# Latents' projections ahead of the low-rank ones, and the recurrence's first seven rounds beside the last two row chunks

## The reference, cut to what matters

```python
h = rms_norm(x, mix_pre_norm) * (1 + sc_m) + sh_m     # x: 1024 tokens x 1024
proj = h @ w_in                                        # 456 attention columns, 1824 recurrent ones
# attention: latents c_q, c_kv, idx_k; score = sum_h w_h relu(q_h . k); keep the best 256 of each row
# recurrence: p + mu_shift * (p_prev - p), split into r, k, v and three low-rank inputs wd, ad, gd
w_log = -softplus(-(w0 + tanh(wd) @ w_decay_up)) - 0.5
a = sigmoid(a0 + ad @ w_aaa_up);  g = sigmoid(gd) @ w_gate_up
S = S * w_t + (S @ a_t) b_t + v_t k_t ;  y_t = S @ r_t          # 8 heads of 64 x 64, 1024 steps
```

## Time and profile before

| | before |
|---|---|
| times of three runs | 3676.62, 3683.32, 3688.82 us; median 3683.32 |
| profiled execution | 3676.93 us, span 3675.6 us |
| PE, DVE, ACT, POOL busy | 3362.3, 1789.6, 931.7, 345.4 us |
| mean granted clock | 0.957 of full |

### The profile page before, as it was taken

One profiled execution on the slowest core, in us unless ns is written; L12 is line 12 of the kernel. 1 busy time (PEld: TensorE's weight loads), 2 busy tenths in 40 slices (PEclk: granted clock), 3 DMA queues, 4 the chain that ended last, 5 costly groups with the idle time before them and its releaser, 6 DMA issues.

```text
span 3675.6 us, 51037 instructions
## 1 busy us (share of the span) xinstructions
PE 3362.3 (91%) x21635; PEld 2614.7 (71%) x21650; DVE 1789.6 (49%) x2849; ACT 931.7 (25%) x1710; POOL 345.4 (9%) x277
## 2 busy tenths in 40 slices
PE   6989757888889999999999889999998999999998
PEld 3757546765557788888886556876676888878876
DVE  2248878663566422223544546322246444444556
ACT  2146532332543300001112435000015111111122
POOL 0000156662000000000000000000000000000000
PEclk8999877988999999999999999999999999999999
DMA  6145411110024111112340101101123111123434
GB/s 210 41 68 183 155 36 37 37 60 19 13 75 138 58 46 52 46 50 94 107 140 25 36 24 35 46 21 49 57 98 117 55 47 46 52 69 98 143 113 145
DMA packets 216068, 270.18 MB, mean 74 GB/s; under 512 B 11068, under 2 KB 176226, under 8 KB 215587
## 3 DMA queue, kind: packets, MB, share of 16 engines
q1 hardware_dynamic: 210555, 247.87, 21.1%
q10 hardware_dynamic: 3192, 11.17, 1.7%
q0 software_dynamic: 2096, 7.87, 0.6%
HBM read 232.80 MB, written 34.08 MB: 73 GB/s over the span
## 4 chain that ended last, share of the span: by engine, by line
PE 80%; DVE 11%; ACT 3%; issue 3%; DMA 2%; POOL 1%; SPq 0%; DVEq 0%; ACTq 0%; POOLq 0%
PE psum L1977 18%; PE psum L1981 18%; PE psum L1979 18%; PE psum L508 5%; PE psum L2995 3%; PE psum L1181 2%; PE psum L2495 2%; PE psum L2816 2%; PE psum L2703 2%; PE psum L552 1%; PE psum L1727 1%; PE psum L2832 1%; DVE scores L913 1%; PE psum L1753 1%; DVE Lg L1821 1%
## 5 line engine op out<-in xcount | busy, mean ns | idle before, releaser
L1977 PE MATMUL psum<-hT_hi,wcut_lo 128*128 128x512 f32 x1856 | 589.9, 395 | 16.8 <-DVE hT_lo L2016 16.8
L1981 PE MATMUL psum<-hT_lo,wcut_hi 128*128 128x512 f32 x1856 | 582.8, 391 | 0.0
L1979 PE MATMUL psum<-hT_hi,wcut_hi 128*128 128x512 f32 x1856 | 582.6, 391 | 0.0
L1977 PEld LDWEIGHTS psum<-hT_hi,wcut_lo 128*128 128x128 f32 x1856 | 350.7, 189 | 97.2 <-DVE hT_lo L2016 17.9
L1959 DVE CAST wcut_hi<-raw 128x1024 fp32r<-128x1024 f32 x256 | 177.1, 692 | 477.0 <-PE psum L1981 453.0
L1979 PEld LDWEIGHTS psum<-hT_hi,wcut_hi 128*128 128x128 f32 x1856 | 350.7, 189 | 73.0
L1981 PEld LDWEIGHTS psum<-hT_lo,wcut_hi 128*128 128x128 f32 x1856 | 350.4, 189 | 73.4
L1977 PE MATMUL psum<-wcut_hi,xcut_lo 128*128 128x512 f32 x1120 | 347.3, 391 | 17.6 <-DVE xcut_lo L2095 13.8
L1981 PE MATMUL psum<-wcut_lo,xcut_hi 128*128 128x512 f32 x1120 | 346.5, 391 | 0.0
L1979 PE MATMUL psum<-wcut_hi,xcut_hi 128*128 128x512 f32 x1120 | 346.2, 390 | 0.0
L1035 POOL TENSOR_TENSOR st<-st,nhalf 128x1 f32<-128x1 f32 (+2 forms) x78 | 61.0, 789 | 2890.0 <-DVE st L676 2890.0
(11 more groups left out here) (427 smaller groups left out, 4396.8 us busy)
## 6 DMA issues: line engine op xcount, KB each, us to landing
raw<-in_w_ffn_down SPq DMA_DIRECT2D x88, 512.0 KB, 3.6
raw<-in_w_ffn_up SPq DMA_DIRECT2D x66, 512.0 KB, 3.8
slot<-in_ada_w SPq DMA_DIRECT2D x24, 1024.0 KB, 11.2
raw<-in_w_in SPq DMA_DIRECT2D x28, 512.0 KB, 5.3
raw<-in_w_ffn_gate SPq DMA_DIRECT2D x22, 512.0 KB, 3.9
slot<-in_w_in SPq DMA_DIRECT2D x8, 1024.0 KB, 6.4
raw<-in_w_out SPq DMA_DIRECT2D x16, 512.0 KB, 3.7
x_one<-xrow SPq DMA_DIRECT2D x16, 512.0 KB, 2.8
```

The source lines that it names most:

```text
L1977: pe.matmul(outs[i], al, bs[i][0], start=start, stop=False, skip_group_check=True)
L1979: pe.matmul(outs[i], ah, bs[i][0], start=False, stop=False, skip_group_check=True)
L1981: mm = pe.matmul(outs[i], ah, bs[i][1], start=False, stop=stop, skip_group_check=True)
```

## The change

The latents' projections now stand ahead of the low-rank ones. "lora" 0 is computed one matmul at a time between the first 16 score steps, "lora" 1 and 2 behind the scores, and DVE runs 30 passes of the search there (`LORA_PASSES`). All 16 modulation steps stand between ("rkv", 1, 5) and ("rkv", 3, 4), one behind each row step, with fixed slots. The last 16 row steps, chunks 4 and 5, have 2 passes each instead of 4, and rounds 0 to 6 of tile 0 stand behind every second of them (`round_beside`). The recurrence's loop begins at round 7. Its rows are loaded in two parts: r and k (`keys_load`), which need chunks 0 to 3 alone, and v (`values_load`). POOL's three operations on v move from a tile's round 1 to round 6 (round 8 for tile 0). The recurrence's constants move up, into `rwkv_weights` behind the load of chunk 4's weights. The last chunk is stored in two halves. Buffers lie elsewhere, so that round 0 can run while the stage buffers and the search are alive, and the attention's first loads all wait for the last inversion (T "U", 7).

```diff
+ROW_LOADS = [("mod", j, q) for j in (0, 1) for q in range(4)] + ["att a", "att b", ("rkv", 0), "idx q", ("rkv", 1), "lora a", "lora b",
+             ("rkv", 2)]
...
-        if _c < 5 and _t in (5, 6, 7)[:3 if _c < 4 else 2]:
-            ROW_STEPS.append(_mods.pop(0))
-ROW_STEPS += _mods
+        if (1, 5) <= (_c, _t) < (3, 5):
+            ROW_STEPS.append(_mods[sum(s[0] == "mod" for s in ROW_STEPS)])
+    _chunk_done.append(sum(s[0] == "mod" for s in ROW_STEPS))
...
+for _i, _s in enumerate(_mods):
+    ROW_LOADS.append(_s)
+    ROW_LOADS += [("rkv", _c + 3) for _c in range(3) if min(_chunk_done[_c] + 2, len(_mods)) == _i + 1]
+SLOT_OF = {_s: (1, 3, 4)[_i % 3] for _i, _s in enumerate(_mods)}
+SLOT_OF.update({("rkv", _c): 2 * (_c % 2) for _c in range(2, 6)})
...
+BESIDE = len(ROW_STEPS) - 2 * NT
...
-        if key == ("rkv", 3):
+        if key == ("rkv", 4):
             rwkv_weights(sp, K)
-        if key == ROW_LOADS[-1]:
-            rwkv_constants(sp, K)
+    rwkv_rows(sp, K)
...
     for n, (t, q) in enumerate(SCORES):
-        score_tensor(pe, K, t, q, SCORE_BANKS[n % 2])
+        score_tensor(pe, K, t, q, n)
+        if n < 16:
+            lora_tensor(pe, K, 0, n)
+    for m in (1, 2):
+        for n in range(16):
+            lora_tensor(pe, K, m, n)
     for i in range(ROWS_FIRST, len(ROW_STEPS) + 1):
...
+        if round_beside(i) is not None:
+            front_tensor(pe, K, 0, round_beside(i))
+
+def round_beside(i):
+    n = i - BESIDE
+    return (n - 3) // 2 if n >= 3 and n % 2 and i < len(ROW_STEPS) else None
...
+LORA_PASSES = 14, 16, 0
...
 def passes_beside(i):
-    return 4 if ROW_STEPS[i - 1][0] == "rkv" else 2
+    return 4 if ROW_STEPS[i - 1][0] == "rkv" and i <= BESIDE else 2
...
 def best_steps(g):
-    return 2 if g < 21 else 1
+    return 3 if g < 14 else 2
...
 def rounds_of():
-    for g in range(STEP * (NT - 1) + LAST):
+    for g in range(STEP, STEP * (NT - 1) + LAST):
...
+    sp.wait_ge(*D["bias"].at("bias"))
+    for i, nme in enumerate(("w0", "a0", "k_k", "k_a", "r_k")):
+        sp.dma_start(K.rowB[:, i, :], wide_row(K, nme)).then_inc(*D["rb"].up("rb", 16))
+    sp.dma_start(K.muB, bcast(I["mu_shift"][0:1, 0:1024], 1024)).then_inc(*D["mu"].up("mu", 16))
...
+def rwkv_rows(sp, K):
+    I, D = K.I, K.D
+    sp.wait_ge(*D["st0"].at(3))
+    sp.wait_ge(*D["st1"].at(2))
+    sp.wait_ge(*D["prows"].at("zero row"))
+    keys_load(sp, K, 0)
...
+VALUES, VALUES_FIRST = 6, 8
...
+    if j == (VALUES if t else VALUES_FIRST):
         g.wait_ge(*D["prev"].at(t))
...
-def rwkv_start(eng, K):
-    fence(eng, K, "proj")
-    eng.wait_ge(*K.D["st0"].at(5))
```

More of the change, by code:

```diff
@@ L130, in __init__, with put @@
         self.n, self.count, self.slot, self.held = n, 0, {}, {}
[L132 to L133 removed]
+    def put(self, key, i=None):
+        i = self.count % self.n if i is None else i
         self.count += 1
@@ L403, in ring_load @@
 def ring_load(sp, K, key, src, kt, cols):
-    i, before = K.ring.put(key)
+    i, before = K.ring.put(key, SLOT_OF.get(key))
     if before is not None:
@@ L541, in proj_tensor @@
     pe.wait_ge(*S.at(("hT", 6)))
-    for m, (key, a, M) in enumerate((("lora a", 0, 128), ("lora a", 128, 128), ("lora b", 0, 32))):
-        w, landed = ring_tile(K, key, 8, 256 if key == "lora a" else 32)
-        b = 2 + 2 * m
-        pe.wait_ge(*landed.at(key))
-        pe.wait_ge(*B.free(b))
-        pe.wait_ge(*B.free(b + 1))
-        p = bank(K, b, 2)
-        for k in range(8):
-            for half in range(2):
-                h = slice(half * 512, (half + 1) * 512)
-                mm = pe.matmul(p[0:M, h], w[:, k, a:a + M], K.hT[:, k, h], start=k == 0, stop=k == 7, skip_group_check=True)
-        mm.then_inc(*T.up(("lora", m)))
-        if m:
-            T.mark(("free", key))
-        B.until(b, S, ("lora", m))
-        B.until(b + 1, S, ("lora", m))
     wa, la = ring_tile(K, "att a", 8, 256)
@@ L598, in proj_tensor, with lora_tensor, score_bank, score_tensor @@
             mod_sum(pe, K, ROW_STEPS[i - 1], ROW_BANK[i - 1])
-SCORE_BANKS = (2, 4), (6, 0)
-def score_tensor(pe, K, t, q, bs):
+        if round_beside(i) is not None:
[3 more added lines that the diff above has]
+    return (n - 3) // 2 if n >= 3 and n % 2 and i < len(ROW_STEPS) else None
+LORA = ("lora a", 0, 128, 6), ("lora a", 128, 128, 2), ("lora b", 0, 32, 4)
+def lora_tensor(pe, K, m, n):
+    key, a, M, b = LORA[m]
+    w, landed = ring_tile(K, key, 8, 256 if key == "lora a" else 32)
+    k, half = divmod(n, 2)
+    h = slice(half * 512, (half + 1) * 512)
+    if n == 0:
+        pe.wait_ge(*landed.at(key))
+    if k == 0:
+        pe.wait_ge(*K.bank.free(b + half))
+    mm = pe.matmul(bank(K, b + half)[0:M, :], w[:, k, a:a + M], K.hT[:, k, h], start=k == 0, stop=k == 7, skip_group_check=True)
+    if n == 15:
+        mm.then_inc(*K.T.up(("lora", m)))
+        if m:
+            K.T.mark(("free", key))
+        K.bank.until(b, K.S, ("lora", m))
+        K.bank.until(b + 1, K.S, ("lora", m))
+def score_bank(n, j):
+    return 2 * ((2 * n + j) % 3)
+def score_tensor(pe, K, t, q, n):
     T, V, S, B = K.T, K.V, K.S, K.bank
+    bs = score_bank(n, 0), score_bank(n, 1)
     W = (t + 1) * 128
@@ L765, in proj_vector @@
     K.best = best_rows(v, K)
+    for m, steps in enumerate(LORA_PASSES):
+        shift_vector(v, K, m)
+        for _ in range(steps):
+            next(K.best)
     for i in range(ROWS_FIRST, len(ROW_STEPS) + 1):
+        if i == ROWS_FIRST + 4:
+            for m in (1, 2):
+                L = K.lora[0:(128, 128, 32)[m], m, :]
+                v.wait_ge(*S.at(("gate tanh", m)))
+                v.tensor_scalar(L, L, 0.5, 0.5, MUL, ADD).then_inc(*V.up())
         for _ in range(passes_beside(i)):
@@ L963, in proj_scalar @@
     s.dma_start(K.ikB, bcast(I["idx_k_norm"][0:1, :], 64)).then_inc(*D["m2"].up("m2", 16))
-    for m, M in enumerate((128, 128, 32)):
-        s.wait_ge(*T.at(("lora", m)))
-        s.activation(K.lora[0:M, m, :], bank(K, 2 + 2 * m, 2)[0:M, :], ACT.Copy).then_inc(*S.up(("lora", m)))
-    for m, M in enumerate((64, 128, 32)):
-        L = K.lora[0:M, m, :]
-        s.wait_ge(*V.at(("shift", m)))
-        s.activation(L, L, ACT.Tanh, scale=0.5 if m else 1.0).then_inc(*S.up(("gate tanh", m)))
     for t in range(NT):
@@ L989, in proj_scalar @@
         for j in range(2):
-            score_scalar(s, K, t, 2 * q + j, SCORE_BANKS[n % 2][j], 2 * n + j)
+            score_scalar(s, K, t, 2 * q + j, score_bank(n, j), 2 * n + j)
+        if n == 16:
+            lora_scalar(s, K, 0)
     K.sums = best_sums(s, K)
+    for m, steps in enumerate(LORA_PASSES):
+        if m:
+            lora_scalar(s, K, m)
+        low_scalar(s, K, m)
+        for _ in range(steps):
+            next(K.sums, None)
     for i in range(ROWS_FIRST, len(ROW_STEPS) + 1):
@@ L996, in proj_scalar, with lora_scalar, low_scalar @@
             next(K.sums, None)
+        if round_beside(i) is not None:
+            front_scalar(s, K, 0, round_beside(i))
+def lora_scalar(s, K, m):
+    M, b = LORA[m][2:]
+    s.wait_ge(*K.T.at(("lora", m)))
+    s.activation(K.lora[0:M, m, :], bank(K, b, 2)[0:M, :], ACT.Copy).then_inc(*K.S.up(("lora", m)))
+def low_scalar(s, K, m):
+    L = K.lora[0:(64, 128, 32)[m], m, :]
+    s.wait_ge(*K.V.at(("shift", m)))
+    s.activation(L, L, ACT.Tanh, scale=0.5 if m else 1.0).then_inc(*K.S.up(("gate tanh", m)))
 def lat_scalar(s, K, step, b):
@@ L1445, in front_tensor @@
         r = half(j)
+        if t == 0 and j == 0:
+            pe.wait_ge(*K.D["mk"].at("mk"))
+            pe.wait_ge(*S.at(("gate tanh", 0)))
         pe.wait_ge(*B.free(7))
```

174 lines of the change are left out of this document (92 added, 82 removed).

## The result

The changed kernel takes 3666.05 us (median of 18 runs, 3662.16 to 3682.6), the kernel before 3675.71 us beside it (18 runs, 3668.31 to 3688.82). The ratio is 0.9976, 95% interval 0.9965 to 0.9988: some 9 us faster. The interval leaves out 1, but the gain is smaller than the 0.3% that I called the bound for a measurable change. Forecast were 3653 us and, by the sum, a gain of 26.5 us. The profiled execution takes 3662.25 us, 14.7 less than that of before, where the sum said 26.5.

A forecast was written before the change was run, and what follows sets the result against it. PE, busy 91% of the span, bounds most stages; the change can take the 44.5 us before round 7. 35 - 11.5 + 3 = 26.5 us gives 3650.4; half of 6.4 us added makes 3653 us, range 3632 to 3672.

The forecast's parts named there:

- The scores begin at 186.1: PE's 48 low-rank matmuls, 44.43 us, leave the path ahead of the scores, which start at 186.1 instead of 230.56.
- 0.93 us just fits ... I add 2.5 us: Score steps: one low-rank matmul fills PE's 1.00 us wait for ACT; 2.5 us extra for narrow steps, ACT's copy, third bank pair.
- DVE behind the scores: Between scores and row steps: DVE's shifts, 30 passes and waits for ACT last from 240.1 to 275; PE is ready at 267.
- Modulation 14's weights, 9 us less 1.5 of backlog: Row steps: weights queued on SP land 25 us after chunk 2; PE waits 9 us, DVE's backlog takes 1.5; chunk 3 ends at 374.
- Rounds 0 to 6 beside 16 row steps, 68 us: Last 16 row steps: 55.2 us plus 6.6 of front matmuls, 5 of waits and 1.3; round 7 starts at 442, 35 us earlier.
- What comes back behind round 7: Rounds 7 to 29: 16 more search passes and tile 0's late v operations make the recurrence 11.5 us later, between 3 and 17.
- Rounds 21 to 29, "I take 6 us" and "2.5 us": Recurrence: 14 passes instead of 7 in rounds 21 to 27 cost 6 us; rounds 28 and 29 cost 2.5 us.
- Tile 0's v operations, 2.5 us: Behind round 7: they stand behind tile 1's mixing on POOL, and PE's second product of round 9 waits: 2.5 us.
- Rounds 7 to 20, 4.5 later and 2.5 earlier: Recurrence: seven more passes in rounds 7 to 13 cost 4.5 us; as many but cheaper in rounds 14 to 20 win 2.5.
- Rival 1: Little is given back: modulation 14's weights come in time, extra passes fill DVE's waits; 44.5 us gain, 3636 us; chance 0.17.
- Rival 2: Rounds 0 to 6 are not hidden: round 3 or 4 waits for POOL's norm, PE stops; 3676 us; chance 0.12.
- Rival 3: Slower: v operations in round 6 hold DVE, ACT and PE's banks, 4.9 us a tile; 3691 us; chance 0.06.

The follow-up runs named there:

- e6: Changed kernel with low-rank group 0 behind the scores, four bank pairs again and the passes ahead of each shift; ratio 0.9968 to the kernel before.
- e4: Changed kernel with the six broadcast loads of the recurrence's constants behind the last modulation weights; ratio 0.9974 to the kernel before.
- e11: Changed kernel with four passes at the first nine of the last 16 row steps, none at the other seven; ratio 0.9927 to the kernel before.
- e5: Changed kernel with POOL's operations on tile 0's v rows in round 6, ahead of tile 1's mixing; ratio 0.9969 to the kernel before.
- e3: Changed kernel with POOL's three v operations back from round 6 to round 1 of tiles 1 to 7; ratio 0.9995 to the kernel before.
- e9: Changed kernel with rounds 0 to 6 of tile 0 behind the row steps again, without passes in them; ratio 1.0014 to the kernel before.

## Why the prediction was off, step by step

**The direction was right, the size not, and the direction partly by luck.** Against a forecast gain of 26.5 us round 7 came 16 us too late, and 14 us more than forecast were lost behind it. Two things that the sum had too small or not at all made up for half of that (below). The gap before round 7 was filled as planned. Round 7 came at 458.2, and I had 442. My own bound for "rounds not hidden" was 455, and it misled: the rounds were beside the row steps, what stood before them was late. Of the 16 us, in the prediction's order:

- *The scores begin at 186.1*: 189.1. Two thirds of the 3 us are in the attention columns, which now follow the cold start directly and take 79.4 us instead of 77.1.
- *"0.93 us just fits ... I add 2.5 us"*: this step failed, in both numbers that it compares. The 1.00 us of wait was the longest of the 16 steps; the mean was 0.62. The 0.93 us was the matmul's share in a row of its own kind; between score steps it takes 1.13. PE's own work (26.4 + 18.0 us) is thus more than the old 36.4, and the scores take 61.1 us in place of 54.0, +7.1. The third bank pair, for which I gave a part of the 2.5 us, is 1.1 us of it in the narrow steps; how much in the others no run shows (e6).
- *DVE behind the scores*: 35 us to the row steps; DVE took 36, and PE then waited 6.60 us for ACT behind it (287.8). In e6 PE itself is late and waits only 0.56 us, but round 0 comes no earlier.
- *Modulation 14's weights, 9 us less 1.5 of backlog*: a wait of 11.03, within the 4 to 14 that I gave, and 2.7 of clock behind it that the sum had not. DVE had no backlog: the pairs with gate rows ran at PE's pace of 5.1 us, not at 5.5, which gave 3 us back. e4 shows the queue's part: 1.8 MB less, 5.9 us less. Chunk 3 ends near 391, not at 374.
- *Rounds 0 to 6 beside 16 row steps, 68 us*: 67.2. The size was right and the reason half so: I named ACT's copies behind its counts in rounds 5 and 6, 2.5 us each; it was one wait of 5.33, behind DVE's and ACT's passes (e11).

**What comes back behind round 7.** I said 11.5 us; by the periods it is 25.8. Of this miss of 14 us two terms make the most.

- *Rounds 21 to 29, "I take 6 us" and "2.5 us"*: 9.5 and 9.7. This step failed in the overlap, not in the work. For rounds 21 to 27 I forecast some 51.5 us of DVE, and it is 50.1; but I took the period to be little longer than DVE's work, and it is 59.2, since DVE's waits do not take the passes up: they are 9.0 us now and were 6.3 before. For rounds 28 and 29 I costed the passes by their number: DVE's work rises by 10.1 us, as the widest tile's last four now stand there together. e11, which ends the search before round 28, brings that period back to 44.3.
- *Tile 0's v operations, 2.5 us*: 4.8 (e5). I had seen that they stand behind tile 1's mixing, and sized the wait at half.
- *Rounds 7 to 20, 4.5 later and 2.5 earlier*: 3.9 and 2.8, both later, the first with the v rows in it.

**What made up for it.** The v operations in round 6 shorten a steady period by 3 us, not 0.5; the three steady periods give 6.8 (e3 takes 6.5 of it back), where the sum had 3 for all. And the recurrence's last stretch is 11.3 us shorter, which nothing in the prediction has: 5.7 of it probably the moved loads, whose place I had costed at nothing, 5.5 the luck of the two profiled executions.

**The rivals.** Rival 1, little given back: no, more was given back than I said. Rival 2, the rounds not hidden: they were, and e9 prices that at 11 us of round 7. Rival 3, slower by the v operations: the opposite, they help. **Costed at nothing**: the attention's loads stayed covered; PE waits 0.84 us for ACT's `mixT` ahead of the attention, as before.

**The rule weighed.** By the rule of the Trainium skill ("SBUF — State Buffer", section "SBUF: two separate sides"), that DVE and GpSimd take their shared port pair in turns, I had worked out that the move of the v operations might only shift collisions, and kept my 3 us against it. The trace has operations as the rule would have them (`Pe` 2.18 us and `Y<-Y,sm` 2.76, where the same size takes 0.69 alone). But e3 shows that the move pays, 3 us in each of two steady periods: what one pair of operations does to each other does not tell what a round costs.
